# The odd layer's normed input laid out in token classes modulo four

## What is computed

```python
DIL_PATTERNS = ((128, 1), (512, 4), (2048, 16))      # (window, dilation)

def odd_mixer(h, w_in, q_gain, k_gain, w_out):
    z = (h @ w_in).reshape(B, S, DIL_GROUPS, 3, DIL_HEADS, DIL_DH)
    q = rmsnorm(z[:, :, :, 0], q_gain)
    k = rmsnorm(z[:, :, :, 1], k_gain)
    v = z[:, :, :, 2]
    for g, (window, dilation) in enumerate(DIL_PATTERNS):
        o_g, lse_g = dilated_branch(q[:, :, g], k[:, :, g], v[:, :, g], dilation, window // dilation)
    ...
    wts = jax.nn.softmax(jnp.stack(lses, axis=0), axis=0)
    o = jnp.sum(wts[..., None] * jnp.stack(outs, axis=0), axis=0)
    return o.reshape(B, S, ODD_MIX) @ w_out
```

## Time and profile before

| | |
|---|---|
| median of 3 runs | 3464.23 us (3464.01 to 3467.14) |
| the profiled execution | 3466.48 us, span 3464.7 us |
| TensorE, matmuls | busy 3362.7 us, 97% |
| TensorE, weight loads | busy 2875.5 us, 83% |
| VectorE | 1788.7 us, 52% |
| ScalarE | 1222.9 us, 35% |
| GpSimd | 1044.7 us, 30% |
| the odd layer up to its attention's end | about 676 to 1030 us of the span |
| mean granted clock of TensorE | 0.988 |

### The profile page before, as it was taken

The page is one execution under the profiler, slowest core; times in us unless marked ns, Lnnn a source line. Parts: engine busy times, 40 slices in busy tenths (PEclk is TensorE's granted clock), DMA queues, the critical chain, the costliest instruction groups (busy, mean ns, idle before and its releaser), DMA issues.

```text
span 3464.7 us, 48089 instructions
## 1 busy us (share of the span) xinstructions
PE 3362.7 (97%) x17856; PEld 2875.5 (83%) x17856; DVE 1788.7 (52%) x2205; ACT 1222.9 (35%) x1582; POOL 1044.7 (30%) x513
## 2 busy tenths in 40 slices
PE   7979999999999999999999999999999999999999
PEld 6758888888888888898888886988888888988887
DVE  5466876532327857546664567565552245262222
ACT  4344433342424423544322246322233222432221
POOL 2112222220212222454443313244423333134332
PEclk9989999999999999999999999999999999999999
DMA  4202433320203433345554330254422243222222
GB/s 151 76 29 80 150 138 125 110 98 25 85 25 132 148 122 133 132 172 175 183 194 146 140 108 13 93 198 172 164 104 97 97 152 126 94 74 97 97 97 97
DMA packets 69899, 402.65 MB, mean 116 GB/s; under 512 B 7520, under 2 KB 10096, under 8 KB 31088
## 3 DMA queue, kind: packets, MB, share of 16 engines
q1 hardware_dynamic: 46400, 318.79, 25.7%
q10 hardware_dynamic: 23344, 81.73, 6.7%
HBM read 398.39 MB, written 2.10 MB: 116 GB/s over the span
## 4 chain that ended last, share of the span: by engine, by line
PE 90%; ACT 3%; DVE 3%; issue 2%; POOL 1%; DMA 1%; SPq 0%; DVEq 0%; ACTq 0%; POOLq 0%
PE banks L485 23%; PE banks L486 23%; PE banks L487 23%; PE banks L397 3%; PE banks L398 3%; PE banks L399 3%; PE banks L502 2%; PE banks L503 2%; PE banks L504 2%; ACT whi L902 2%; PE banks L591 1%; PE banks L555 1%; DMA raw<-stream 1%; POOL wlo L2089 1%; PE banks L814 1%
## 5 line engine op out<-in xcount | busy, mean ns | idle before, releaser
L2089 POOL TENSOR_TENSOR wlo<-raw,whi 128x512 fp32r<-128x512 f32 x283 | 721.0, 2548 | 2059.2 <-ACT whi L902 2044.8
L485 PE MATMUL banks<-h_hi,whi 128*128 128x512 f32 (+1 forms) x2752 | 1043.5, 379 | 14.8 <-POOL wlo L2089 7.7
L487 PE MATMUL banks<-h_hi,wlo 128*128 128x512 f32 (+1 forms) x2752 | 1035.2, 376 | 0.0
L486 PE MATMUL banks<-h_lo,whi 128*128 128x512 f32 (+1 forms) x2752 | 1035.1, 376 | 0.0
L902 ACT ACTIVATE whi<-raw 128x2048 fp32r<-128x2048 f32 x281 | 536.8, 1910 | 530.0 <-PE banks L487 526.2
L1404 DVE TENSOR_TENSOR wlo<-raw,whi 128x1536 fp32r<-128x1536 f32 x281 | 523.3, 1862 | 312.2 <-ACT whi L902 311.9
L485 PEld LDWEIGHTS banks<-h_hi,whi 128*128 128x128 f32 x2752 | 519.1, 189 | 116.2 <-issue 20.8
L486 PEld LDWEIGHTS banks<-h_lo,whi 128*128 128x128 f32 x2752 | 519.1, 189 | 96.0 <-issue 3.4
L487 PEld LDWEIGHTS banks<-h_hi,wlo 128*128 128x128 f32 x2752 | 519.1, 189 | 94.0
L485 PE MATMUL banks<-mid_hi,whi 128*128 128x512 f32 (+1 forms) x1136 | 424.6, 374 | 6.1 <-POOL wlo L2089 5.0
L486 PE MATMUL banks<-mid_lo,whi 128*128 128x512 f32 (+1 forms) x1136 | 423.8, 373 | 0.0
(11 more groups left out here) (274 smaller groups left out, 4120.3 us busy)
## 6 DMA issues: line engine op xcount, KB each, us to landing
raw<-stream SPq DMA_DIRECT2D x299, 1024.0 KB, 4.8
mraw<-mod_stream ACTq DMA_DIRECT2D x144, 512.0 KB, 3.4
x<-xT SPq DMA_DIRECT2D x8, 256.0 KB, 5.5
out<-x SPq DMA_DIRECT2D x8, 256.0 KB, 2.1
ka<-k_a ACTq DMA_DIRECT2D x1, 1600.0 KB, 6.5
ko<-k_odd ACTq DMA_DIRECT2D x1, 1152.0 KB, 5.2
crow<-c_rows ACTq DMA_DIRECT2D x1, 1024.0 KB, 6.3
cx<-ctxT SPq DMA_DIRECT2D x1, 1024.0 KB, 7.5
```

The source lines that it names most:

```text
L485: mm(o, hi, a_hi[:, kc, 0:T], start=(kc == 0), stop=False)
L486: mm(o, hi, a_lo[:, kc, 0:T], start=False, stop=False)
L487: last = mm(o, lo, a_hi[:, kc, 0:T], start=False, stop=(kc == K - 1))
L2089: G.tensor_tensor(wlo[:, slot, WD:], raw[:, slot, WD:], whi[:, slot, WD:].bitcast(F32), ALU.subtract)\
```

## The change

The norm `mix1` is written class by class: column r*128 + n of `h_hi` and `h_lo` holds token 4n + r. A half of the tokens (256) is then four runs of 64 columns instead of one of 256. The scale step reads the residual and the norm's factor at a stride of four elements and writes the staging buffer in class order; the high and low parts are written as four runs. The first pair's products read those runs and write their accumulators in the same pattern. All later readers of `h_hi` and `h_lo` in this layer see class order; value slabs of all three groups take consecutive tiles, score products consecutive queries and keys, and the mask of group 0 is made for keys in class order. The other norms keep their order.

```diff
+IN_CLASSES = ("mix1",)
+def half_cols(norm, row, a):
+    if norm not in IN_CLASSES:
+        return row[:, a:a + HS]
+    return row.rearrange("p (r n) -> p r n", r=4)[:, :, a // 4:(a + HS) // 4]
+def by_class(norm, run):
+    return run.rearrange("p (n r) -> p r n", r=4) if norm in IN_CLASSES else run
+def class_blocks(norm, run):
+    return run.rearrange("p (r n) -> p r n", r=4) if norm in IN_CLASSES else run
...
-                    last = three(acc[s % 2][j][:, at:at + HS], h[:, w], lo[:, w], a_hi[:, kc, at:at + HS],
-                                 a_lo[:, kc, at:at + HS], kc == 0, kc == K - 1)
+                    last = three(half_cols(order, acc[s % 2][j], at), h[:, w], lo[:, w],
+                                 half_cols(order, a_hi[:, kc, :], at), half_cols(order, a_lo[:, kc, :], at),
+                                 kc == 0, kc == K - 1)
...
-                    cls = [slice(t * P, (t + 1) * P) if g == 0 else slice(t, S, 4) for t in range(4)]
-                    slab_tokens(s + 6 + g, (s + 6 + g) % 2, cls)
+                    slab_tokens(s + 6 + g, (s + 6 + g) % 2, toks)
...
-                    masked(dst[0], oq[:, hh, r:S:4], okk[:, hh, :], 0, ko_r[:, KO_NEAR + r * S:KO_NEAR + (r + 1) * S])
+                    masked(dst[0], oq[:, hh, r * P:(r + 1) * P], okk[:, hh, :], 0, ko_r[:, KO_NEAR + r * S:KO_NEAR + (r + 1) * S])
-                        last = masked(dst[1][:, (g - 1) * P:g * P], oq[:, 2 * g + hh, r:S:4],
-                                      okk[:, 2 * g + hh, r:S:4], 0, ko_r[:, k:k + P])
+                        last = masked(dst[1][:, (g - 1) * P:g * P], oq[:, 2 * g + hh, r * P:(r + 1) * P],
+                                      okk[:, 2 * g + hh, r * P:(r + 1) * P], 0, ko_r[:, k:k + P])
...
+                dst, y = half_cols(norm, h_hi[:, c, :], a), class_blocks(norm, stgh[:, u % 4, :])
-                    A(h_hi[:, c, a:b], stgh[:, u % 4, :], ACT.Copy).then_inc(hi_done, 1)
+                    A(dst, y, ACT.Copy).then_inc(hi_done, 1)
...
-                V.scalar_tensor_tensor(out=stgh[:, u % 4, :], in0=res[TOKENS[norm]][:, c, a:b], scalar=norm_scale(norm, c),
-                                       in1=rstd[:, RSTD_SLOT[norm], a:b], op0=ALU.mult, op1=ALU.mult)\
+                V.scalar_tensor_tensor(out=class_blocks(norm, stgh[:, u % 4, :]),
+                                       in0=by_class(norm, res[TOKENS[norm]][:, c, a:b]), scalar=norm_scale(norm, c),
+                                       in1=by_class(norm, rstd[:, RSTD_SLOT[norm], a:b]), op0=ALU.mult, op1=ALU.mult)\
...
-                    V.tensor_tensor(h_lo[:, c, a:b], y, hi, ALU.subtract).then_inc(lo_done, 1)
+                    V.tensor_tensor(dst, y, hi, ALU.subtract).then_inc(lo_done, 1)
...
-        dist = (r + 4 * p)[:, None] - t[None]
+        dist = (r + 4 * p)[:, None] - (4 * (t % P) + t // P)[None]
```

More of the change, by code:

```diff
@@ L399, in three, with half_out @@
                 return mm(o, lo, r_hi, start=False, stop=end)
-            def half_out(s, kc, K, js, a_hi, a_lo, at):
+            def half_out(s, kc, K, js, a_hi, a_lo, at, order=None):
                 h, lo = w_hi(s), w_lo(s)
@@ L442, in first_pair @@
                     for i in range(2):
-                        half_out(n0 + i, kc, DC, js[i], h_hi, h_lo, 0)
+                        half_out(n0 + i, kc, DC, js[i], h_hi, h_lo, 0, norm)
                     if norm in HALVED and kc == 4:
@@ L449, in first_pair @@
                             unit_ready(norm, 8 + kc)
-                        last = half_out(n0 + i, kc, DC, js[i], h_hi, h_lo, HS)
+                        last = half_out(n0 + i, kc, DC, js[i], h_hi, h_lo, HS, norm)
                     last.then_inc(slab_done, 1)
@@ L948, in unit_hi @@
                 shift = norm_shift(norm, c)
+                dst, y = half_cols(norm, h_hi[:, c, :], a), class_blocks(norm, stgh[:, u % 4, :])
                 if shift is None:
-                    A(h_hi[:, c, a:b], stgh[:, u % 4, :], ACT.Copy).then_inc(hi_done, 1)
+                    A(dst, y, ACT.Copy).then_inc(hi_done, 1)
                 else:
-                    A(h_hi[:, c, a:b], stgh[:, u % 4, :], ACT.Identity, bias=shift).then_inc(hi_done, 1)
+                    A(dst, y, ACT.Identity, bias=shift).then_inc(hi_done, 1)
             def halved(norm, then=None):
@@ L1444, in unit_lo @@
                 dve.wait_ge(hi_done, SPLIT[norm][0] + u + 1)
-                y, hi, shift = stgh[:, u % 4, :], h_hi[:, c, a:b].bitcast(F32), norm_shift(norm, c)
+                y, hi = class_blocks(norm, stgh[:, u % 4, :]), half_cols(norm, h_hi[:, c, :], a).bitcast(F32)
+                dst, shift = half_cols(norm, h_lo[:, c, :], a), norm_shift(norm, c)
                 if shift is None:
-                    V.tensor_tensor(h_lo[:, c, a:b], y, hi, ALU.subtract).then_inc(lo_done, 1)
+                    V.tensor_tensor(dst, y, hi, ALU.subtract).then_inc(lo_done, 1)
                 else:
-                    V.scalar_tensor_tensor(out=h_lo[:, c, a:b], in0=y, scalar=shift, in1=hi, op0=ALU.add,
-                                           op1=ALU.subtract).then_inc(lo_done, 1)
+                    V.scalar_tensor_tensor(out=dst, in0=y, scalar=shift, in1=hi, op0=ALU.add, op1=ALU.subtract)\
+                        .then_inc(lo_done, 1)
             def units(norm):
```

## The result

The changed kernel takes 3412.64 us in the median (3412.02 to 3416.76, 4 runs) against 3465.68 for the kernel before, measured beside it (3464.01 to 3467.14, 4 runs): 53.0 us less, ratio 0.9851 with a 95% interval of 0.9839 to 0.9863. The forecast was 3412.3. The profiled execution took 3412.39 us with a span of 3410.6.

What follows compares the result with a forecast made beforehand. TensorE, busy 97% of the span, was taken as the bound. Value slabs 43.5 us and scores 8.4 us, with costs 0, made 51.9 us less than the median 3464.23: 3412.3 us, range 3408 to 3421.

Steps and rivals of the forecast that it cites:

- The value slabs: Odd layer, groups 1 and 2: 384 matmuls go from 0.2333 to 0.1200 us each without the stride, 43.5 us less.
- Warm scores: Attention of the odd layer, 2 passes of 6 units at full clock: each score 0.63 us shorter, 7.6 us less.
- lower bound 0.49: Least gain per warm attention unit in us, counting only strided weight loads that stand uncovered, 0.12 us for each.
- six short steps: End of a unit's scores, mask products included: 1.18 us before, priced at 0.112 us each with contiguous operands.
- Cold units: First two units of each attention pass, partly at granted clock 0.50: 4 units win 0.2 us each, 0.8 us.
- rival B: Attention: shorter scores give nothing because the exchange with VectorE and ScalarE ends last; only 43.5 us won, 3420.7 us, chance 0.06.
- The scale step: VectorE's norm step, 16 times, reading at a stride of four: 0.19 us more each, hidden, cost 0, at most 2.2 us.
- over 0.21 more: Sign in the first pair: a gap ahead of the second half's last units means the scale step costs over 0.21 us more.
- First pair's operands in runs: 192 matmuls of the first pair reading and writing four runs of 64 columns: cost 0, at most 21.7 us.
- C: Rival, first pair: the broken accumulator slows products toward 0.233 us, up to 21.7 us comes back, 3434.0 us; chance 0.09.
- D: Rival, value slabs of groups 1 and 2: something other than stride keeps them at 0.233 us, 3455.8 us; chance 0.03.
- E: Rival, first pair: four-run access costs over 0.27 us per product, slower than before, 3466 us at 0.40 spacing; chance 0.02.

## Why the prediction was right

*The value slabs* (43.5 forecast, 43.32 in the table, 44.9 in the timed run with this part undone). The step that carries the result was to take the distance of starts from a group whose instructions differ in nothing but the stride, and to check that nothing else is late at the new pace. Nothing was.

*Warm scores* (7.6 forecast, 7.9 measured). From unit 2's first matmul (rows below) to the end of the attention the first pass went from 854.94 - 824.17 = 30.77 us to 828.16 - 801.32 = 26.84, 3.93 less; the second from 1028.92 - 998.11 = 30.81 to 975.65 - 948.81 = 26.84, 3.97 less. The choice of 0.63 over the lower bound 0.49 rested on a guess, "the strided moving operand seems to cost as well", and the two runs show it: queries 0.49, keys 0.42. A unit gained 0.66 rather than 0.63, since two of the "six short steps" are mask products of 128 columns, which I priced at 0.112 us like the others. They take 0.06, and did so before (chain of waits):

```profile
842.27 0.06 PE banks L593
```

*Cold units* (0.8 forecast, 1.8 measured). This term was mis-sized. TensorE's instructions at the first pass's start are units 0, 1 and 2. Before (TensorE's timeline):

```profile
817.24 2.07 PE L591 MATMUL banks<-okk,oq 128*128 128x512 f32 x2 [6.71 <-DVE ko_r L1888]
...
820.74 2.02 PE L591 MATMUL banks<-okk,oq 128*128 128x512 f32 x2
...
824.17 1.17 PE L591 MATMUL banks<-okk,oq 128*128 128x512 f32 x2
```

And in the changed kernel, with unit 2 of the second pass behind them:

```profile
795.33 2.05 PE L612 MATMUL banks<-okk,oq 128*128 128x512 f32 x2 [6.70 <-DVE ko_r L1911]
...
798.77 1.36 PE L612 MATMUL banks<-okk,oq 128*128 128x512 f32 x2
...
801.32 1.12 PE L612 MATMUL banks<-okk,oq 128*128 128x512 f32 x2 [0.34 <-ACT oP L1139]
...
948.81 1.13 PE L612 MATMUL banks<-okk,oq 128*128 128x512 f32 x2 [0.75 <-ACT oP L1139]
```

Units 0 and 1 took 6.93 us and take 5.99, with a wait of 0.34 us for ScalarE's exponential included, which is new: there the exchange with the helpers ends last, as rival B said of the whole stage. In the second pass it is 6.96 and 6.11, with a wait of 0.75. Unit 0 alone, all of it at a granted clock of 0.50, went only from 3.50 to 3.44 us, where I had forecast 0.2 less: its six short steps take 1.19 us on the chain (797.80 to 798.99) and not the 1.06 that I had worked out for half rate. Nearly all of the gain is in unit 1, part of which now runs at full clock. Busy time by stretch of one microsecond each, before, from 4.8 us after unit 0's start (granted clock is the third number from the end):

```profile
822.00:823.00 1.00, 1.00 (x3) 0.39 (x3) 0.13 (x1) 0.76 (x1) 0.00 (x0) 0.52 0.00 0
...
823.00:824.00 1.00, 1.00 (x7) 0.98 (x5) 0.00 (x0) 0.24 (x2) 0.00 (x0) 1.00 0.00 0
```

The changed kernel, from 2.7 us after that start:

```profile
798.00:799.00 1.00, 1.00 (x7) 1.00 (x6) 0.00 (x0) 0.00 (x0) 0.00 (x0) 0.50 0.20 82
...
799.00:800.00 1.00, 1.00 (x3) 0.43 (x4) 0.96 (x1) 0.00 (x0) 0.00 (x0) 0.83 0.00 0
```

Counted from unit 0's start, the half clock lasted 5.7 us before and 4.0 after; in the second pass 5.9 and 3.4. I had assumed that it covers the same two units. It does not follow the scores' strides. In the runs with strided queries and with strided keys it ended 4.5 and 3.2 us after unit 0's start in the first pass. And the run with strides of two and three in the value slabs, whose attention is the changed kernel's line for line, has 5.7 and 5.9 us, as long as before the change. Its timeline (units 0 and 2) and busy time:

```profile
802.40 2.04 PE L612 MATMUL banks<-okk,oq 128*128 128x512 f32 x2 [6.71 <-DVE ko_r L1913]
...
808.70 1.07 PE L612 MATMUL banks<-okk,oq 128*128 128x512 f32 x2
...
807.00:808.00 1.00, 1.00 (x3) 0.47 (x2) 0.19 (x2) 0.66 (x1) 0.00 (x0) 0.50 0.00 0
```

Its units 0 and 1 take 6.30 us, and 6.40 in the second pass. So with the half clock as long as before, the contiguous operands are worth 6.93 - 6.30 = 0.63 and 6.96 - 6.40 = 0.56 us, 1.2 together against the 0.8 forecast; the other 0.6 us of the 1.8 came with the shorter half clock. That part is luck as far as the change goes: over all traces with this attention behind the same gaps the half clock ended between 2.9 and 6.1 us after unit 0's start. What sets its length is not shown.

*The scale step* (0.19 more forecast, 0.20 measured; cost forecast 0, measured 0.26 on the pair). The size was right and the cover was misjudged. VectorE's timeline for units 8 and 15, and the chain's two lengthened products, in the changed kernel:

```profile
685.07 0.68 DVE L1458 SCALAR_TENSOR_TENSOR stg<-x,par,rstd 128x256 f32<-128x256 f32 x1 [1.83 <-ACT rstd L952]
...
691.58 0.68 DVE L1458 SCALAR_TENSOR_TENSOR stg<-x,par,rstd 128x256 f32<-128x256 f32 x1
...
691.98 0.18 PE banks L417
...
692.76 0.34 PE banks L417
```

VectorE is idle 1.83 us before unit 8 instead of 3.28, so the first half is covered, as forecast. In the second half I compared the delay of eight steps, 1.5 us, with the slack of unit 15, 1.68 us. But unit 14's split also waits for eight scale steps, since it is queued behind unit 15's, and TensorE asks for it 0.72 us sooner. Its slack was 1.53 us (ready at 691.53, asked for at 693.06), and the eight steps take 1.6. The two products that wait are those of units 13 and 14, by 0.06 and 0.22 us. Even this accounting is short by about 0.2 us in both units. By it unit 13, delayed by seven steps of 0.2 against a slack of 1.54, would be in time by 0.14, and unit 14, with TensorE itself 0.06 late by then, would make it wait 0.01. Both comparisons take a unit as usable at the moment its split ends; that the missing 0.2 is the way from there to TensorE's start is likely, but no run shows it. So the sign that the prediction gave for this gap, "over 0.21 more" for the step, was set too high as well.

*First pair's operands in runs* (0 forecast, 0 measured; up to 21.7 feared). Spacing 0.120 with runs of 64, and the run with whole halves has the same two short waits in the pair and nothing else.

*The rivals.* B came true for one wait in each pass, 0.34 and 0.75 us; C, D and E not at all. Against the sum the cold units won 1.0 us more and the warm scores 0.3 more, while the pair lost 0.3 and the slabs won 0.2 less, so the table ends 0.85 over the forecast. The timed difference of 53.0 against 51.9 is inside what such runs scatter (3412.02 to 3416.76). That 3412.3 came so near to 3412.64 is in part chance: the 1.1 us won beyond the forecast meet a kernel before that stood 1.45 us higher beside the result (3465.68) than where the forecast began (3464.23). The chances hold a slip: E has 0.02, but "same" and "slower", which only E gives, have 0.03 together.

## What to carry to other kernels

A stationary operand at a stride of four float32 elements makes a chain of short matmuls run at the pace of its loads: look for two groups of the same instruction whose starts lie differently far apart, and lay the data out for the reader that is met most often. The stride then moves to a writer or a reader that has slack; check that slack for every item in the queue behind the slower step, not for the last alone. And where a stage begins behind a gap, what is won in the gap's last waits (here 6.6 us by waiting for less, against 9.7 from the faster attention) can be worth nearly as much as the stage's own speed.

## What the runs showed of the hardware that was not expected

- Load of 128 float32 columns: 192 ns in order, 195 at a stride of two, 261 at three, 329 at four, and starts 0.120, 0.120, 0.173 and 0.233 us apart.
- The moving operand: 256 columns take 0.120 us in order or in four runs, 0.143 with every element 512 bytes from the last (four runs in turn), 0.234 at a stride of 16 bytes inside each run. Here a small regular stride is dearer than far jumps, with the same 16 bytes read again after 16 elements in the one and after 4 in the other.
- The accumulator: runs of two columns cost nothing, 0.120.
- VectorE, 256 float32 elements in a scale step: 478 ns in order, 679 with one input at a stride of four, 680 with both.
- The half clock behind the gaps of 6.6 and 4.3 us lasted between 2.9 and 6.1 us from the first matmul in kernels with the same attention, and a wait of 2.1 us inside an attention was followed by another 3.5 us at 0.51.
